# A transformer kernel whose first mixer keeps its tokens by grid columns, so that neighbourhood attention scores 128 queries with two key blocks and the context

## The chip, the cores and the metric

The kernel runs on one core of one Trainium2 chip. A core has five engines that run their own instruction streams and wait for each other by semaphores: TensorE (PE: matrix products into PSUM), VectorE (DVE), ScalarE (ACT), GpSimd (POOL) and SyncE (SP, which only issues DMAs here). The metric is the device time of one execution in microseconds, lower is better. The kernel before takes 2480.74 us, the median of 3 runs (2480.32 to 2481.86).

## What is computed

Two blocks follow one another on 512 tokens of width 1024. The second has two layers; it also carries 256 context tokens. The change touches the mixer of its first layer (`even_mixer`), which runs two attentions on halves of the width:

```python
qa, ka, va, qb, kb, vb = split(h @ w_in)               # 512 latent tokens and 256 context tokens
ya = neighbourhood_attention(rms(qa), rms(ka), va, ka_ctx, va_ctx, rpb)     # 8 heads of 64
yb = diff_attend(rope(rms(qb)), rope(rms(kb)), vb, ...)                     # 4 pairs of heads, all 768 keys
y  = concat([ya, rms(yb)]) @ w_out

# neighbourhood_attention: the 512 tokens are a grid of 8 rows and 64 columns, token = 64*row + column
row_start = clip(row - 4, 0, 8 - 8)                    # = 0: the window takes all 8 rows
col_start = clip(col - 8, 0, 64 - 16)                  # 16 columns
s = concat([q . k[window] * scale + rpb[row offset, column offset], q . k_ctx * scale])
out = softmax(s) @ concat([v[window], v_ctx])
```

So a latent query sees 8 x 16 = 128 latent keys, in a band of grid columns, and all 256 context keys. The context tokens attend to the 256 context keys alone.

## The kernel before

Activations lie with the channels on the 128 partitions and the tokens along the free dimension: 8 tiles of 512 latent and 256 context columns (`T` = 768). Dense layers multiply weights and activations in three products of high and low parts (lines 274 to 276 and, for the values, 356 to 358). Weight units stream through a ring of 4 slots: SP loads them (L3075), ACT makes the high part (L267), POOL the low part (L3124).

The program goes through stages in a fixed order that all engines follow by hand-written waits. Around the change these are: modulation `mod_a0` (DVE scales x at L595, ACT adds the shift at L611, DVE makes the low part at L589; PE multiplies tile by tile as they come, L274 to L276), the projection of the diff half (`Projection`, DVE rotates with `rope_vector` L631 to L633 and divides by the norm L755 to L760, values leave PSUM at L380), its attention, the projection of the neighbourhood half, its attention, the product with `w_out_e`, and the residual update (L1274).

Neighbourhood attention is `RowTiledAttention` over 24 "pairs". A pair is 128 queries of two heads, one head on each half of the partitions. For each of the 4 head pairs `t` there are six in this order: two blocks of context queries against 256 keys, then four blocks of latent queries against all 768 keys. With tokens by rows every block of 128 queries (two grid rows) needs all 512 latent keys; what lies outside the window is masked by the bias table. So 256 of the 768 key columns are context and 384 of the other 512 are masked for each query.

The steps of pair `p`, by engine:
- PE `score` (L1072): one product for each head and 256 keys, into PSUM. The profile counts two records for each product in fp32.
- DVE `largest` (L1180 and L1182): the maximum. A wide pair takes two instructions for each head: 256 context columns with a zero bias, then 512 with the bias table.
- ACT `exp` (L1148), DVE reciprocal (L1168), POOL scaling of the probabilities (L1015).
- PE `turn` (L1090): transposes into PSUM banks 6 and 7, which hold one phase of at most 8 blocks; ACT copies them out (L1136). A pair of 12 blocks turns in two phases, the first ("opening") at step `p+2`, the second ("closing") at step `p+3`. Each turn waits until the phase before is copied.
- PE `sum` (L1109): values times probabilities, at step `p+4`; DVE stores the result (L1187).

One step of the PE loop is: `sum(p-4)`, closing turn of `p-3`, `score(p)`, opening turn of `p-2`. In a wide pair `score` also waits before its second chunk for the store of pair `p-4`. DVE at its step `p` does `largest(p)` for head 0, the reciprocals of `p-1`, the store of `p-3` and `largest(p)` for head 1; ACT does its first exp, then the closing copy, then its second exp. After some steps DVE also prepares the bias table of a head (L1718: 14 x 64 = 896 columns, at the first two pairs of each `t`) or a lower part of the mix (L1251), and ACT its high part (L1244). At the end PE fills in three products with `w_out_e` beside the last pairs. The bias tables come by 16 DMAs of 64 partitions x 14 rows x 256 bytes (L3175), 12 of them issued after the projection.

Of the kernel before, what the change touches and what calls it, by code (L numbers as in the profile page):

```python
# [14 lines left out]
P = 128  # L15
D = 1024
DT = D // P
S = 512
# [12 lines left out]
WIN_R, WIN_C = 8, 16  # L31
EMB, ORDER = 33, 64
# [29 lines left out]
for _name, _n in PARAMS:  # L62
# [6 lines left out]
          ("later", P), ("upto", P), ("na_mask", GRID_W), ("cos", S), ("sin", S)]  # L69
# [512 lines left out]
def modulate_vector(k, v, name, layer, shift0, lo, n):  # L582
# [46 lines left out]
def rope_vector(k, v, x, xs, gain, gain_swap):  # L629

    link(v, v.eng.scalar_tensor_tensor(x, x, gain, k.const("cos", 0, S), ALU.mult, ALU.mult))  # L631
    link(v, v.eng.scalar_tensor_tensor(xs, xs, gain_swap, k.const("sin", 0, S), ALU.mult, ALU.mult))
    v.eng.tensor_tensor(x, x, xs, ALU.add).then_inc(k.sem("head_rotated"), 1)  # L633


class Projection:
# [5 lines left out]
    def __init__(self, k, name, tiles, values, units, width, dst, before, evacuated, rotated, turned, jobs):  # L642
# [3 lines left out]
        self.evac, self.backward = k.sem("head_evac"), turned  # L646
# [42 lines left out]
    def scalar(self, s):  # L689
        k, n = self.k, self.tiles  # L690

        def square(i):
# [8 lines left out]
            blocks = (lambda ap: ap.rearrange("p (b n) -> p b n", n=P)) if i < self.backward else (lambda ap: ap)  # L701
            back = (lambda ap: blocks(ap)[:, :, ::-1]) if i < self.backward else (lambda ap: ap)
            s.eng.activation(back(k.sq[:, i % 2, 0:size]), blocks(src), ACT.Square).then_inc(self.squares, 1)

        def keep(i):
# [8 lines left out]
            if i < self.backward:  # L714
                x, src = x.rearrange("p (b n) -> p b n", n=P)[:, :, ::-1], src.rearrange("p (b n) -> p b n", n=P)
# [27 lines left out]
    def vector(self, v):  # L743
        k, n = self.k, self.tiles
        for events in self.slots:
            for j in events:
                x, _, gain, _, _, gain_swap = self.jobs[j]
                size = x.shape[-1]
                if gain_swap is not None:
                    v.eng.wait_ge(self.evac, self.e + j + 1)  # L750
                    rope_vector(k, v, x[:, 0:S], swapped(k, j), gain, gain_swap)
# [15 lines left out]
class PairAttention:  # L767
# [5 lines left out]
    def __init__(self, k, pairs, third, before, opened, wide=(0, 0, 0)):  # L773
# [9 lines left out]
        self.wide = [sum(it["keys"].shape[-1] > S for it in pairs[:p]) for p in range(len(pairs) + 1)]  # L783
# [27 lines left out]
    def score_at(self, p, h):  # L811

        base = 1536 * (p % 2)
        return base if h == 0 else base + (768 if self.pairs[p]["keys"].shape[-1] > S else 512)

    def probs(self, p, h):
        n = self.pairs[p]["keys"].shape[-1]
# [23 lines left out]
    def score(self, pe, p):  # L841
        k, it = self.k, self.pairs[p]
        self.open(pe, "score", p)
        n = it["keys"].shape[-1]
# [32 lines left out]
    def sum(self, pe, p):  # L877
# [6 lines left out]
        for b, val in enumerate(it["values"]):  # L884
            if it["joined"]:
                last = pe.matmul(k.ps[:, out:out + P], val, self.probs_turned(p, b, b + 1), start=b == 0, stop=b == n - 1)
            else:
                for h in range(2):
                    r, g = slice(HD * h, HD * h + HD), h * n + b
                    last = pe.matmul(k.ps[r, out:out + P], val[:, r], self.probs_turned(p, g, g + 1), start=b == 0,  # L890
# [27 lines left out]
    def scalar(self, s, between=None):  # L918
# [8 lines left out]
        def exp(p, h):  # L927
            it, n = self.pairs[p], self.pairs[p]["keys"].shape[-1]
# [19 lines left out]
    def vector(self, v, between=None):  # L948
# [12 lines left out]
        def largest(p, h):  # L961
            it, n, at = self.pairs[p], self.pairs[p]["keys"].shape[-1], self.score_at(p, h)
# [5 lines left out]
            w, least = it["bias"][h].shape[-1], -MASKED  # L968
# [54 lines left out]
class RowTiledAttention(PairAttention):  # L1023
# [31 lines left out]
    def score(self, pe, p):  # L1055
        k, it = self.k, self.pairs[p]
        self.open(pe, "score", p)
        n = it["keys"].shape[-1]
# [5 lines left out]
        for a in range(0, n, CTX):  # L1064
            b = min(a + CTX, n)
# [4 lines left out]
            for h in range(2):  # L1070
                r, at = slice(HD * h, HD * h + HD), self.score_at(p, h)
                last = pe.matmul(k.ps[:, at + a:at + b], it["q"][r], it["keys"][r, a:b], start=True, stop=True)  # L1072
# [2534 lines left out]
```

## Time and profile before

| | us |
|---|---|
| median of 3 runs | 2480.74 |
| profiled execution, span | 2478.6 |
| mod_a0 with its first products | 767 to 787 |
| diff projection | 787 to 883 |
| diff attention | 883 to 966 |
| neighbourhood projection | 966 to 1082 |
| neighbourhood attention | 1082 to 1175 |
| product with w_out_e | 1175 to 1242 |

The times of the stages are microseconds from the start of the span, read off the timeline. The profile shows one execution: "busy" is the time in which an engine had an instruction under way. PE records overlap (a matmul's record lasts longer than the distance to the next), so a group of matmuls is best read by its first start and the next group's start. PEclk is the clock that TensorE was granted, as a share of 2.4 GHz.

### The profile page before, as it was taken

What the parts mean: (1) busy time and instruction counts of PE and PEld (TensorE: products, weight loads), DVE (VectorE), ACT (ScalarE), POOL (GpSimd) and SP (SyncE); (2) the same over time, 40 slices, a digit from 0 to 9 for tenths busy, and PEclk for the clock granted to TensorE, in tenths of its full rate; (3) what the DMA queues carried; (4) which work ended last, traced back from release to release, by engine and by line L of the source; (5) the groups of instructions that cost most, each with busy time, mean ns of one, the idle gap of its engine ahead of it and who ended that gap; (6) DMA issues with size and microseconds to landing.
All of it is one profiled execution on the core that took longest, in us unless ns stands there. A gap on an engine that the chain in (4) does not pass through costs nothing.

```text
span 2478.6 us, 37835 instructions
## 1 busy us (share of the span) xinstructions
PE 2426.4 (98%) x14711; PEld 1982.5 (80%) x14711; DVE 1512.1 (61%) x2120; ACT 974.5 (39%) x1541; POOL 829.5 (33%) x446
## 2 busy tenths in 40 slices
PE   8999999999999999999999999999999999999999
PEld 6778877888886877777888888888887757788887
DVE  6765755458567975696366866644777587424242
ACT  4576643232325455357242122132256332423232
POOL 2533033544441222233223323232223322354443
PEclk9999999999999999999999999999999999999999
DMA  6222023445431101130123433322311111233232
GB/s 248 86 68 77 3 68 126 146 144 172 151 127 41 53 26 33 52 79 2 60 94 114 158 127 126 121 94 91 129 62 56 53 67 54 83 114 97 94 102 85
DMA packets 78682, 228.53 MB, mean 92 GB/s; under 512 B 21568, under 2 KB 23616, under 8 KB 77898
## 3 DMA queue, kind: packets, MB, share of 16 engines
q1 hardware_dynamic: 65176, 177.12, 21.9%
q10 hardware_dynamic: 13362, 49.40, 6.0%
q8 instruction: 102, 1.67, 0.3%
q14 instruction: 42, 0.34, 0.0%
HBM read 224.37 MB, written 2.12 MB: 91 GB/s over the span
## 4 chain that ended last, share of the span: by engine, by line
PE 84%; DVE 7%; issue 4%; ACT 2%; POOL 2%; DMA 0%; SPq 0%; DVEq 0%; POOLq 0%; ACTq 0%
PE ps L274 23%; PE ps L275 23%; PE ps L276 22%; PE ps L1109 2%; PE ps L1072 2%; POOL w_lo L3124 1%; PE ps L1090 1%; PE ps L856 1%; DVE rstd L755 1%; PE ps L873 1%; PE ps L358 1%; PE ps L356 1%; PE ps L357 1%; PE ps L468 1%; PE ps L2896 1%
## 5 line engine op out<-in xcount | busy, mean ns | idle before, releaser
L3124 POOL TENSOR_TENSOR w_lo<-ring,w_hi 128x1024 fp32r<-128x1024 f32 x288 | 703.5, 2443 | 1163.9 <-ACT w_hi L267 661.1
L274 PE MATMUL ps<-act_hi,w_hi 128*128 128x512 f32 x2280 | 843.6, 370 | 4.8 <-DVE act_lo_mixer L589 2.4
L276 PE MATMUL ps<-act_hi,w_lo 128*128 128x512 f32 x2280 | 828.6, 363 | 0.0
L275 PE MATMUL ps<-act_lo_ffn,w_hi 128*128 128x512 f32 (+1 forms) x1408 | 512.9, 364 | 0.0
L274 PEld LDWEIGHTS ps<-act_hi,w_hi 128*128 128x128 f32 x2280 | 429.1, 188 | 93.0 <-issue 16.5
L276 PEld LDWEIGHTS ps<-act_hi,w_lo 128*128 128x128 f32 x2280 | 428.1, 188 | 71.9
L267 ACT CAST w_hi<-ring 128x1024 fp32r<-128x1024 f32 (+1 forms) x167 | 172.6, 1034 | 653.8 <-PE ps L276 604.7
L1471 ACT CAST w_hi<-ring 128x1024 fp32r<-128x1024 f32 (+1 forms) x132 | 137.6, 1043 | 457.4 <-PE ps L276 457.4
L1363 DVE SCALAR_TENSOR_TENSOR ada_place<-ada_place 128x1024 f32<-128x1024 f32 x180 | 284.6, 1581 | 25.4 <-DMA ada_place<-in_w_ada 10.5
L275 PEld LDWEIGHTS ps<-act_lo_ffn,w_hi 128*128 128x128 f32 x1408 | 265.1, 188 | 41.1
L274 PE MATMUL ps<-hidden_hi,w_hi 128*128 128x512 f32 x704 | 256.5, 364 | 1.8 <-DVE hidden_lo L1554 1.5
L275 PE MATMUL ps<-hidden_lo,w_hi 128*128 128x512 f32 x704 | 256.5, 364 | 0.0
L276 PE MATMUL ps<-hidden_hi,w_lo 128*128 128x512 f32 x704 | 255.2, 363 | 0.0
L1554 DVE TENSOR_TENSOR hidden_lo<-probs,hidden_hi 128x512 f32 (+3 forms) x66 | 150.0, 2273 | 63.7 <-ACT hidden_hi L1497 63.7
L1552 DVE TENSOR_TENSOR probs<-probs,ps 128x512 f32<-128x512 f32 (+1 forms) x66 | 51.3, 777 | 208.4 <-PE ps L276 200.7
L274 PEld LDWEIGHTS ps<-hidden_hi,w_hi 128*128 128x128 f32 x704 | 132.6, 188 | 25.0 <-DVE hidden_lo L1554 2.4
L276 PEld LDWEIGHTS ps<-hidden_hi,w_lo 128*128 128x128 f32 x704 | 132.3, 188 | 21.9
L275 PEld LDWEIGHTS ps<-hidden_lo,w_hi 128*128 128x128 f32 x704 | 132.6, 188 | 20.5
L275 PE MATMUL ps<-act_lo_mixer,w_hi 128*128 128x512 f32 (+1 forms) x416 | 147.3, 354 | 0.0
L1539 DVE SCALAR_TENSOR_TENSOR probs<-ps,params,probs 128x511 f32<-128x511 f32 x66 | 43.6, 661 | 133.0 <-ACT probs L1486 132.0
L755 DVE RECIPROCAL rstd<-probs 128x768 f32<-128x768 f32 x20 | 99.0, 4949 | 41.8 <-ACT probs L732 41.7
L1591 DVE SCALAR_TENSOR_TENSOR x_res<-ps,mod,x_res 128x512 f32<-128x512 f32 x72 | 47.7, 662 | 124.5 <-PE ps L276 123.3
(446 smaller groups left out, 3311.2 us busy)
## 6 DMA issues: line engine op xcount, KB each, us to landing
ring<-in_w_ffn SPq DMA_DIRECT2D x204, 512.0 KB, 3.3
ada_place<-in_w_ada ACTq DMA_DIRECT2D x90, 512.0 KB, 4.1
ring<-in_w_gdn SPq DMA_DIRECT2D x16, 512.0 KB, 3.3
ring<-in_w_hy SPq DMA_DIRECT2D x12, 512.0 KB, 3.3
ring<-in_w_dil_qk SPq DMA_DIRECT2D x8, 512.0 KB, 8.7
ring<-in_w_out SPq DMA_DIRECT2D x8, 512.0 KB, 3.3
ring<-in_w_diff_qk SPq DMA_DIRECT2D x8, 512.0 KB, 3.3
ring<-in_w_na_qk SPq DMA_DIRECT2D x8, 512.0 KB, 3.2
```

What stands on the lines that cost most here:

```text
L267: s.eng.copy(k.w_hi[:, u % SPLITS, rest], k.ring[:, u % SLOTS, rest]).then_inc(k.hi_done, 1)
L274: pe.matmul(out, w[0], x[0], start=start, stop=False)
L275: pe.matmul(out, w[0], x[1], start=False, stop=False)
L276: return pe.matmul(out, w[1], x[0], start=False, stop=stop)
L755: link(v, v.eng.reciprocal(k.rstd[:, 0:size], k.probs[:, j % 2, 0:size]))
L1072: last = pe.matmul(k.ps[:, at + a:at + b], it["q"][r], it["keys"][r, a:b], start=True, stop=True)
L1109: last = pe.matmul(k.ps[r, out:out + P], val[:, r], self.probs_turned(p, g, g + 1), start=b == 0, stop=b == n - 1)
L1363: ins = v.eng.scalar_tensor_tensor(k.ada[:, 4, :], k.ada[:, 2 + n % 2, :], 1.0, k.ada[:, q, :], ALU.mult, ALU.mult, accum_out=k.mod_flat[: ...
L1471: s.eng.copy(k.w_hi[:, (u + j) % SPLITS, rest], k.ring[:, (u + j + 2) % SLOTS, rest]).then_inc(k.hi_done, 1)
L1552: v.eng.tensor_tensor(tmp[:, 0:n], tmp[:, 0:n], k.ps[:, val:val + n], ALU.mult).then_inc(f.hidden, 1)
L1554: v.eng.tensor_tensor(k.hid_lo[:, it * 2 + a, 0:n], tmp[:, 0:n], k.hid_hi[:, it * 2 + a, 0:n].bitcast(F32), ALU.subtract).then_inc(f.ready, 1)
L3124: pool.tensor_tensor(k.w_lo[:, a % SPLITS, :], k.ring[:, a % SLOTS, :], k.w_hi[:, a % SPLITS, :].bitcast(F32), ALU.subtract).then_inc(k.lo ...
```

## The change

Before the first layer's mixer the latent tokens are put in column order (token = 8*column + row): `modulate_vector` reads x and the norm by columns and writes them contiguously, RoPE reads its cosine and sine tables by columns, and the residual update reads the product from PSUM back into row order. The context tokens stay. In this order 128 queries starting at token 64 + 128*i are 16 grid columns, and their windows lie within 32 grid columns, that is 256 keys. The latent queries of a head pair become three blocks of 128 against 256 + 256 keys, and one pair that holds the first 64 and the last 64 queries, each half against its own 128 keys and the 256 context keys (384 in all). One instruction now takes the maximum over latent and context keys, with a bias table that holds zeros for the context. The tables (5 x 256 columns for two heads) are laid out on the host and come in one DMA for each `t`. The reversed order of queries that the old table needed is gone. A pair of 4 or 3 blocks turns in one phase (8 or 6 blocks), at step `p+3`.

```diff
@@ modulate_vector
+    turned = name == "mod_a0"
     for t in range(DT):
         for q, (a, b) in enumerate(parts):
-            ins = v.eng.scalar_tensor_tensor(bufs[t % 3][:, a:b], k.x[:, t, a:b], k.mod[:, layer, shift0 + 8 + t, q:q + 1],
-                                             norm_rstd(k, v, name, q), ALU.mult, ALU.mult)
+            dst, src, rstd = bufs[t % 3][:, a:b], k.x[:, t, a:b], norm_rstd(k, v, name, q)
+            if turned and q == 0:
+                dst, src, rstd = in_columns(dst), by_columns(src), by_columns(rstd)
+            ins = v.eng.scalar_tensor_tensor(dst, src, k.mod[:, layer, shift0 + 8 + t, q:q + 1], rstd, ALU.mult, ALU.mult)
@@ rope_vector
+    cos, sin = k.const("cos", 0, S), k.const("sin", 0, S)
+    if columns:
+        cos, sin, x, xs = by_columns(cos), by_columns(sin), in_columns(x), in_columns(xs)
@@ Projection: squares and copies of the queries no longer reverse blocks of 128
@@ RowTiledAttention.score
-        for a in range(0, n, CTX):
-            b = min(a + CTX, n)
+        for c, (a, b) in enumerate(zip([0] + it["ends"], it["ends"])):
...
             for h in range(2):
                 r, at = slice(HD * h, HD * h + HD), self.score_at(p, h)
-                last = pe.matmul(k.ps[:, at + a:at + b], it["q"][r], it["keys"][r, a:b], start=True, stop=True)
+                for rows, q, keys in it["pieces"]:
+                    last = pe.matmul(k.ps[rows, at + a:at + b], q[r], keys[c][r], start=True, stop=True)
@@ RowTiledAttention.sum
-                last = pe.matmul(k.ps[r, out:out + P], val[:, r], self.probs_turned(p, g, g + 1), start=b == 0, stop=b == n - 1)
+                for cols, v in val:
+                    last = pe.matmul(k.ps[r, out + cols.start:out + cols.stop], v[:, r], self.probs_turned(p, g, g + 1)[:, cols],
+                                     start=b == 0 and cols.start == 0, stop=b == n - 1, skip_group_check=len(it["pieces"]) > 1)
@@ largest
+            bias = it["bias"][h]
+            if len(bias.shape) == 3:
+                chunks = lambda ap: ap.rearrange("p (a n) -> p a n", n=bias.shape[-1])
+                v.eng.tensor_tensor_reduce(chunks(self.probs(p, h)), chunks(k.ps[:, at:at + n]), bias, 1.0, -MASKED,
+                                           ALU.add, ALU.min, self.small(p, 0, h)).then_inc(self.maxed, 1)
+                return
@@ residual_vector
+            if name == "w_out_e" and q == 0:
+                x, src = x.rearrange("p (r c) -> p r c", c=GRID_W), back_in_rows(src)
@@ new helpers
+def by_columns(ap):
+    return ap.rearrange("p (r c) -> p c r", c=GRID_W)
+def in_columns(ap):
+    return ap.rearrange("p (c r) -> p c r", c=GRID_W)
+def back_in_rows(ap):
+    return ap.rearrange("p (c r) -> p r c", c=GRID_W)
+def na_table(k, t):
+    return k.view(k.mix_flat, 5 * T, 5, CTX) if t == 0 else k.view(k.big, 12 * T + 5 * CTX * t, 5, CTX)
@@ na_pairs
-        for i in (4, 5, 0, 1, 2, 3):
...
-                out.append(pair(q[:, t, blk], key[:, t, 0:T], vals, k.mix[:, 4 + t, blk][:, ::-1],
-                                bias=[bias[2 * t + h][:, at:at + S] for h in range(2)]))
+        for i in (4, 5):
+            blk = slice(i * P, (i + 1) * P)
+            out.append(pair(q[:, t, blk], ctx, vals[4:], mix[:, blk], bias=[k.par("zero").broadcast_to([P, CTX])] * 2))
+        for i in range(3):
+            blk = slice(HD + i * P, HD + (i + 1) * P)
+            out.append(pair_of([(slice(0, P), q[:, t, blk], [key[:, t, i * P:i * P + CTX], ctx])], whole[i:i + 2] + whole[4:],
+                               mix[:, blk], bias=[table[:, 0::3, :], table[:, 1:4:2, :]]))
+        low, high, units = slice(0, HD), slice(HD, P), table.rearrange("p a (u n) -> p (a u) n", n=P)
+        out.append(pair_of([(low, q[:, t, 0:HD], [key[:, t, 0:P], ctx]), (high, q[:, t, S - HD:S], [key[:, t, S - P:S], ctx])],
+                           [[(low, vals[0]), (high, vals[3])]] + whole[4:], ...))
@@ na_mask_vector
-        link(v, v.eng.scalar_tensor_tensor(bias, bias, -1.0,
-                                          k.const("na_mask", 0, GRID_W).unsqueeze(1).broadcast_to([P, 14, GRID_W]),
-                                          ALU.mult, ALU.add))
+            edges = na_table(k, t)[:, 2, :]
+            link(v, v.eng.tensor_scalar(edges, edges, -1.0, None, ALU.mult))
+        bias = na_table(k, t)[:, h, :].rearrange("p (c r) -> p c r", c=WINDOW)
+        link(v, v.eng.scalar_tensor_tensor(bias, bias, -1.0, spread(k.const("na_mask", 0, WINDOW), ROWS_ALL), ALU.mult, ALU.add))
@@ load_na_bias
-    for h in (2 * t, 2 * t + 1):
-        for a in range(2):
-            sp.dma_start(na_bias(k)[h][GRID_W * a:GRID_W * (a + 1), :, :],
-                         bass.AP(k.dram["rpb"], (h * 15 + a) * wide, [[1, GRID_W], [wide, 14], [1, GRID_W]]))
+    sp.dma_start(na_table(k, t), k.dram["na_bias"][t]).then_inc(k.sem(f"na_bias_{t}"), 16)
```

## Rows read from the trace of the kernel before

**Rows 1.** The page: the span
```profile
span 2478.6 us, 37835 instructions
```
**Rows 2.** Windows: start:end, length, busy time by engine, PEclk, DMA share, GB/s
```profile
1108.28:1129.95 21.67, 19.24 (x284) 14.69 (x282) 17.19 (x63) 18.14 (x36) 9.03 (x13) 1.00 0.01 2
1129.95:1151.17 21.22, 19.17 (x283) 14.65 (x282) 16.30 (x62) 17.52 (x35) 9.10 (x13) 1.00 0.01 3
```
**Rows 3.** The chain that ended last, in order of time: start, us, what
```profile
1092.40 0.66 PE ps L1109 x8
...
1129.95 1.35 PE ps L1072 x12
...
1139.09 0.59 PE ps L1090 x12
...
1142.18 1.46 PE ps L1109 x24
...
1173.60 1.46 PE ps L1109 x24
```
**Rows 4.** Timeline, turns on PE and their copies on ACT: start, us, what
```profile
1133.70 0.56 ACT L1136 COPY pair_turned<-ps 128x512 f32<-128x512 f32 x1
...
1134.46 0.45 PEld L1109 LDWEIGHTS ps<-pair_turned,big 128*64 128x64 f32 x8 [0.36 <-ACT pair_turned L1136]
...
1150.59 0.59 PE L1090 MATMUL ps<-consts,act_place 64*128 64x64 f32 x12
...
1151.21 0.80 ACT L1136 COPY pair_turned<-ps 128x768 f32<-128x768 f32 x1 [0.68 <-PE ps L1090]
...
1153.91 0.46 PE L1090 MATMUL ps<-consts,probs 64*128 64x64 f32 x8
```
**Rows 5.** Groups by form, 1084 to 1174: names, shapes, count, busy, mean ns, idle before
```profile
L1148 ACT ACTIVATE act_place<-act_place,small 128x768 f32<-128x768 f32 x16 | 15.0, 939 | 4.9 <-DVE small L1182 4.8
L1148 ACT ACTIVATE probs<-probs,small 128x256 f32<-128x256 f32 x8 | 4.1, 512 | 0.1
L1182 DVE CUSTOM_DVE_ANT_0 act_place<-ps,big,small 128x512 f32<-128x512 f32 x12 | 9.0, 751 | 0.4
L1180 DVE CUSTOM_DVE_ANT_0 act_place<-ps,params 128x256 f32<-128x256 f32 x16 | 6.7, 419 | 3.2 <-PE ps L1072 2.0 <-DVE big L1718 1.0
```
**Rows 6.** Timeline, the first bias tables on DVE and POOL beside them
```profile
1084.18 2.37 POOL L3124 TENSOR_TENSOR w_lo<-ring,w_hi 128x1024 fp32r<-128x1024 f32 x1 [7.52 <-ACT w_hi L267]
...
1084.41 3.08 DVE L1718 SCALAR_TENSOR_TENSOR mix<-mix,consts 128x896 f32<-128x896 f32 x1
...
1088.34 1.21 DVE L1718 SCALAR_TENSOR_TENSOR mix<-mix,consts 128x896 f32<-128x896 f32 x1
```
**Rows 7.** DVE forms of the whole span: a strided PSUM read, and L595 of mod_a0
```profile
L3051 DVE SCALAR_TENSOR_TENSOR mix<-ps,small,mix 128x512 f32<-128x512 f32 x4 | 3.0, 744 | 0.1
L595 DVE SCALAR_TENSOR_TENSOR sq<-x_res,mod,ps 128x512 f32<-128x512 f32 x24 | 17.9, 744 | 4.6 <-PE ps L458 4.5
L595 DVE SCALAR_TENSOR_TENSOR sq<-x_res,mod,ps 128x256 f32<-128x256 f32 x18 | 8.5, 475 | 0.0
```
**Rows 8.** The same kind of window over mod_a0 and its first products
```profile
767.00:787.00 20.00, 18.81 (x96) 14.77 (x95) 18.80 (x32) 9.38 (x17) 1.35 (x1) 1.00 0.01 1
```
**Rows 9.** Timeline of DVE in the diff projection
```profile
811.31 2.10 DVE L759 TENSOR_TENSOR big<-big,rstd 128x512 f32<-128x512 f32 x1
...
876.60 0.69 DVE L380 COPY big<-ps 128x512 f32<-128x512 f32 x1 [5.08 <-PE ps L358]
```
**Rows 10.** Timeline, the end of the attention, and DVE in the product after it
```profile
1175.43 2.70 DVE L1251 TENSOR_TENSOR mix_lo<-mix,act_hi 128x768 fp32r<-128x768 f32 x3
...
1205.82 1.27 DVE L1274 SCALAR_TENSOR_TENSOR x_res<-ps,mod,x_res 128x512 f32<-128x512 f32 x2 [4.07 <-PE ps L276]
```
**Rows 11.** Windows where the granted clock fell
```profile
249.00:252.00 3.00, 1.10 (x14) 0.47 (x9) 2.74 (x3) 2.41 (x6) 0.00 (x0) 0.93 0.00 0
252.00:255.00 3.00, 3.00 (x42) 2.11 (x42) 2.93 (x3) 0.93 (x4) 0.00 (x0) 0.50 0.00 0
```

More of the change, by code:

```diff
@@ L31 @@
 WIN_R, WIN_C = 8, 16
+WINDOW = 32
+ROWS_ALL = S // GRID_W
+assert WIN_R == ROWS_ALL
 EMB, ORDER = 33, 64
@@ L782, in __init__ @@
         self.joined = [sum(it["joined"] for it in pairs[:p]) for p in range(len(pairs))]
-        self.wide = [sum(it["keys"].shape[-1] > S for it in pairs[:p]) for p in range(len(pairs) + 1)]
+        self.wide = [sum(it["n"] > S for it in pairs[:p]) for p in range(len(pairs) + 1)]
         count, N = dict(self.first), len(pairs)
@@ L843, in score @@
         self.open(pe, "score", p)
-        n = it["keys"].shape[-1]
+        n = it["n"]
         if p >= 2:
@@ L927, in exp @@
         def exp(p, h):
-            it, n = self.pairs[p], self.pairs[p]["keys"].shape[-1]
+            it, n = self.pairs[p], self.pairs[p]["n"]
             if h == 0 and p >= 3:
@@ L961, in largest @@
         def largest(p, h):
-            it, n, at = self.pairs[p], self.pairs[p]["keys"].shape[-1], self.score_at(p, h)
+            it, n, at = self.pairs[p], self.pairs[p]["n"], self.score_at(p, h)
             if it["bias"] is None:
@@ L1057, in score @@
         self.open(pe, "score", p)
-        n = it["keys"].shape[-1]
+        n = it["n"]
         if p >= 2:
@@ L1063, in score @@
                 pe.wait_ge(self.maxed, 2 * self.nth(p - 1))
-        for a in range(0, n, CTX):
-            b = min(a + CTX, n)
+        for c, (a, b) in enumerate(zip([0] + it["ends"], it["ends"])):
             if a == S:
@@ L1071, in score @@
                 r, at = slice(HD * h, HD * h + HD), self.score_at(p, h)
-                last = pe.matmul(k.ps[:, at + a:at + b], it["q"][r], it["keys"][r, a:b], start=True, stop=True)
+                for rows, q, keys in it["pieces"]:
+                    last = pe.matmul(k.ps[rows, at + a:at + b], q[r], keys[c][r], start=True, stop=True)
             if a == 0 and n > S:
@@ L1097, in sum @@
         self.copies_ready(pe, self.phases[p][-1].copies)
-        if p + 2 < len(self.pairs) and self.pairs[p + 2]["keys"].shape[-1] > S:
+        if p + 2 < len(self.pairs) and self.pairs[p + 2]["n"] > S:
             if self.pairs[p + 2]["bias"] is None:
@@ L1141, in exp @@
         def exp(p, h):
-            it, n = self.pairs[p], self.pairs[p]["keys"].shape[-1]
+            it, n = self.pairs[p], self.pairs[p]["n"]
             if h == 0 and p >= 3:
@@ L1170, in largest @@
         def largest(p, h):
-            it, n, at = self.pairs[p], self.pairs[p]["keys"].shape[-1], self.score_at(p, h)
+            it, n, at = self.pairs[p], self.pairs[p]["n"], self.score_at(p, h)
             if it["bias"] is None:
@@ L1641, in pair, with pair_of @@
 def pair(q, keys, values, out, bias=None, factor=None):
-    return dict(q=q, keys=keys, values=values, blocks=len(values), out=out, bias=bias, factor=factor,
-                joined=factor is not None)
+    chunks = [keys[:, a:min(a + CTX, keys.shape[-1])] for a in range(0, keys.shape[-1], CTX)]
+    return pair_of([(slice(0, P), q, chunks)], [[(slice(0, P), val)] for val in values], out, bias, factor)
+def pair_of(pieces, values, out, bias, factor=None):
+    return dict(pieces=pieces, ends=list(itertools.accumulate(ap.shape[-1] for ap in pieces[0][2])), n=len(values) * P, values=values,
+                blocks=len(values), out=out, bias=bias, factor=factor, joined=factor is not None)
 def dil_pairs(k):
@@ L1666, in na_pairs @@
 def na_pairs(k):
     q, key, val = attn_views(k)
[L1668 removed]
+    out = []
     for t in range(4):
[L1670 to L1678 removed]
+        vals, mix, table = [val[:, b, t * P:(t + 1) * P] for b in range(6)], k.mix[:, 4 + t, :], na_table(k, t)
+        whole, ctx = [[(slice(0, P), v)] for v in vals], key[:, t, S:T]
+        for i in (4, 5):
[7 more added lines that the diff above has]
+        out.append(pair_of([(low, q[:, t, 0:HD], [key[:, t, 0:P], ctx]), (high, q[:, t, S - HD:S], [key[:, t, S - P:S], ctx])],
+                           [[(low, vals[0]), (high, vals[3])]] + whole[4:],
+                           mix[:, 0:S].rearrange("p (e n) -> p e n", n=HD)[:, ::S // HD - 1, :], bias=[units[:, 4:9:2, :], units[:, 5:10:2, :]]))
```

88 lines of the change are left out of this document (41 added, 47 removed).

## The prediction

> **What bounds the kernel now.** I read the page first: the span is 2478.6 us [rows 1], the median of the runs 2480.74, so 2.1 us lie outside the span; I keep them and make the sum against the span. The change touches four stages, so I read windows and timelines of those. In neighbourhood attention one group of six pairs takes 21.67 and then 21.22 us, with PE busy for 19.2, ACT for 17.5 to 18.1 and DVE for 16.3 to 17.2 of it [rows 2]. PE leads, but the others stand close behind: removing PE work alone would buy little, and what matters is that the change shrinks the work of all of them. The chain in order of time [rows 3] then gives PE's parts: a score of 768 keys 1.35 us, a turn of 6 blocks 0.59, a sum of 12 blocks 1.46; a context pair has a turn of 0.46 [rows 4] and a sum of 0.66 [rows 3]. From the first sum at 1092.40 to the end of the last at 1173.60 + 1.46 = 1175.06 there are 82.7 us, 24 steps of the PE loop. This is the stretch to be rebuilt.
>
> **Neighbourhood attention, PE.** An interior pair scores 512 columns instead of 768 (0.90 us), turns 8 blocks in one phase (16 records instead of 12 and 12: 0.79) and sums 8 instead of 12 blocks (0.97). The pair of edges scores 384 columns, turns 6 blocks (0.59) and sums 6 (0.73). Its score consists of products on a quarter of the array; if quarters don't overlap it costs up to 1.28, and I show below that this is covered. Context pairs stay: 0.45, 0.46, 0.62 to 0.66.
>
> **What PE waits for in a step.** The turn's PSUM region is free, and the sum has its input, only after ACT's copy. A turn that ended at 1151.18 was followed by the copy at 1151.21, and a copy that ended at 1134.26 by the sum's first load at 1134.46 [rows 4]: 0.03 + copy + 0.20. The copies of 512 and 768 columns took 0.56 and 0.80 [rows 4], 0.94 ns for a column, so 1024 columns cost 1.04. Round trips are thus 0.79, 1.04 and 1.27 us. Only the score lies beside them. A step is sum + turn + the larger of score and round trip. After the change, by p modulo 6:
> - 0 and 1: 0.97 + 0.79 + 1.27 = 3.03 each
> - 2: 0.97 + 0.59 + 1.04 = 2.60
> - 3: 0.73 + 0.46 + 0.90 = 2.09
> - 4: 0.62 + 0.46 + 0.90 = 1.98
> - 5: 0.62 + 0.79 + 1.27 = 2.68 (the edge score, even at 1.28, fits beside the copy)
>
> That is 15.4 us a group. The same reckoning for before (with the second turn and its wait for the first copy) gives 3.68 twice, 3.40, 3.27, 3.02 and 3.15, together 20.2, where the trace has 21.2 to 21.7 [rows 2]; it leaves out 1.0 to 1.5 us of couplings between engines, so I price these for after by themselves. Steps 4 and 5 of the first group (4.66), three groups (46.2) and the tail (steps 24 to 27, each with a product of w_out_e of about 1.27 where the score was: 3.03, 3.03, 2.83, 0.73) make 60.5 us against 82.7: 22.2 less.
>
> **Couplings.** ACT: exps of 768 and 256 columns take 0.94 and 0.51 [rows 5], so 512 take 0.72; its step with two of them and the large copy is 2.5 us, below 3.03. DVE: 419 + 751 ns for each head become one instruction over 512 columns, 751 ns [rows 5], about 0.80 with its accumulator read; reciprocals and store take some 0.5 a step (what maxima, two tables of 1.09 and a low part leave of DVE's 17.19 us a group [rows 2], over six), so a step is 2.1. POOL was busy 9.03 us for the 7168 columns of a group [rows 2], so an interior pair takes 1.3; the turn is now always two steps behind the exps and finds it done, where the opening turn of before waited for it. The weak place is step 3 of the groups in which DVE makes a lower part of the mix (2.70 us for three [rows 10], so 0.9 to 1.1 beside its 2.1) while PE's steps are only 2.0: the next maximum comes late, the exp after it stands ahead of the large copy on ACT, and behind that copy PE waits. Written out, the copy starts 1.3 us late. Two groups have this; the others lose about 0.25, and ACT's casts of the mix in two places 0.35 each. Sum: 2 x 1.3 + 2 x 0.25 + 2 x 0.35 = 3.8 us back.
>
> **Fill.** The first two bias tables took DVE 3.08 and 1.21 us; the first ran into POOL's low part, which ended at 1084.18 + 2.37 = 1086.55 [rows 6]. The new table work is 256 + 256 columns and then 256; it will still have to wait for POOL, and ends perhaps 0.2 us sooner, the second 0.7, and the following pair saves 0.56 on its maxima. The first sum starts about 1.4 us sooner. Later tables shrink as well, within DVE's steps counted above.
>
> The attention comes to -22.2 - 1.4 + 3.8 = -19.8 us. Next late behind it is the product with w_out_e. It starts with tiles prepared long before; DVE's last three low parts took 2.70 us from 1175.43 [rows 10] and move with the end of the attention. Its weights were in the ring by then (the DMA is idle from 1108 on [rows 2]), so the gain isn't eaten there.
>
> **mod_a0.** DVE is busy for 18.80 of the 20 us [rows 8] and PE's products follow it tile by tile, so every nanosecond on its 8 instructions of L595 is exposed. They now read x and the norm with a hop of 64 words at each element. A row shows that a hop at every element in PSUM costs nothing: L3051 takes 744 ns for 512 columns, just as the contiguous L595 [rows 7]. No row shows such a read from SBUF. One bound is therefore 0. The other: a column costs (744 - 475) / 256 = 1.05 ns [rows 7], and if each took two turns, 0.54 us for each of 8 instructions, 4.3 us. I take the middle, 2.1, since x hops in SBUF and the norm in PSUM. The Trainium skill (Vector Engine (DVE) Microarchitecture Reference, Measured stream behaviour on trn2) says that hopping one source at every element raises 1.054 to 1.73 ns for a column, and stepping both by 24 words to 2.50; by it the eight would cost an estimated 2.8 to 5.9 us. No run here shows it yet.
>
> **Cover elsewhere.** RoPE: two of three instructions in 8 jobs now hop in SBUF, at worst 2 x 0.54 = 1.1 us a job. In each job the multiplication L759 takes 2.10 us, where the copy of as many columns takes 0.69 [rows 9], because it runs beside POOL's low part, so up to 1.4 us of delay vanish there; and after the last job DVE idles 5.08 us before the values [rows 9]. I cost it at nothing; without that cover it would be 8.6 us minus 5. The residual reads PSUM with a hop (nothing, by rows 7), and DVE waits 4.07 us for PE there anyway [rows 10]. Squares and copies without the reversal, and 3 DMAs instead of 12 on SP: nothing, since the queue isn't waited for.
>
> **The sum.** -19.8 + 2.1 = -17.7: span 2460.9, time 2480.74 - 17.7 = 2463.0 us.
>
> **Rivals.**
> - *The steps don't follow PE but the loop between engines* (store, maximum, exp, copy, sum runs over two steps). For it speaks that before was 1.0 to 1.5 us a group above PE's reckoning. If after loses 2.5 us a group beyond it (18 us instead of 15.4) the saving is 22.2 + 1.4 - 4 x 2.5 = 13.6, less mod_a0: -11.5, 2469.2. Chance 0.22.
> - *A hop in SBUF costs more than a second turn*: with three turns an element, 8 x 1.08 = 8.6 us in mod_a0, and RoPE at 2.2 us a job breaks its cover of 1.4 by 0.8 x 8 = 6, of which the 5.08 of idle time hide most: -19.8 + 8.6 + 1 = -10.2, 2470.5. Chance 0.09. The Trainium skill's upper figure (same page and section) stands between this and my bound.
> - *More than forecast*: couplings vanish and the hops are free, -22.2 - 1.4 = -23.6, 2457.1; if PE's parts overlap a little more, 2455. Chance 0.1.
> - *Slower: TensorE's clock falls.* PE is busy 90% now; after it would be 13.4 of 16.4 us, 82%, with gaps of up to 0.4 us at each large copy. In this trace the granted clock fell to 0.50 (1.2 GHz) in the three microseconds after a window in which PE was busy for 1.10 of 3 us [rows 11]. If gaps bring it down and it stays, PE work doubles: the stretch holds about 54 us of it, so it costs 54 us minus the waits that it hides (12), against 20 saved: +22, 2503. It decides from about 40% of the stretch at the lower level. Against it: no gap here comes near that one. Chance 0.03.
> - *The gain is eaten*: the product with w_out_e waits for weights or low parts, within 5 us of before. Rows 10 and the idle DMA speak against it. Chance 0.05.
>
> **Numbers.** The forecast has 0.50. Its own range, from the bounds of the hops and 3 us on the couplings either way, is 2458 to 2468. The 8 in 10 take in the first rival: 2456 to 2471. About 0.2%, 5 us, is what a measurement here can tell. Faster by more: 0.91, same 0.05, slower 0.04.
>
> **What would show it.** Right: groups of six pairs in 15.4 to 16.5 us; the turn of 16 records at 0.79 followed by a copy of 1.04 and a PE gap of some 0.3; first sum near 1091 plus the shift of mod_a0; L595 at about 1.0 us; the RoPE stage unchanged in length because L759 shrinks by what L631 and L632 grow; w_out_e of the same length. Wrong: steps of equal length near 3 us (the loop), PEclk below 1.00 in the attention, PE idle before L274 of w_out_e, or a longer diff projection.

## The result, and the profile after

The changed kernel takes 2461.49 us (median of 4, 2459.59 to 2464.36), the kernel before 2481.19 beside it: a ratio of 0.9922 (0.991 to 0.9933), 19.7 us faster where 17.7 were forecast. The profiled execution is the slowest of the four, 2464.36 us with a span of 2462.4.

The window of the kernel after from the first sum's start to the last sum's end (columns as in [rows 2]):

```profile
1093.05:1154.38 61.33, 53.30 (x803) 39.27 (x803) 41.04 (x165) 50.87 (x116) 26.81 (x44) 1.00 0.07 29
```

The 82.66 us of before are now 61.33, a group takes 16.06 us twice and then 15.08 instead of the 21.2 and 21.7 of [rows 2], and the clock stays at 1.00. The chain that ended last, in order of time (start, us, what), has the two kinds of step in it:

```profile
1117.73 0.66 PE ps L1101 x16
1118.42 1.02 ACT pair_turned L1149
1119.48 1.09 PE ps L1121 x16
1120.58 0.52 PE ps L1101 x12
1121.10 0.92 PE ps L1083 x8
1122.02 0.87 PE ps L1121 x16
1123.28 0.95 PE ps L1083 x8
1124.39 0.48 issue
1125.12 1.38 POOL act_place L1026 x2
1126.55 0.65 issue
1127.21 0.54 DVE pair_probs L1193
1127.99 0.81 ACT pair_probs L1161 x2
1128.80 0.91 ACT pair_turned L1149
1129.75 1.09 PE ps L1121 x16
1130.85 0.66 PE ps L1101 x16
1131.53 1.02 ACT pair_turned L1149
1132.59 1.09 PE ps L1121 x16
```

L1121 is the sum, L1101 the turn, L1149 ACT's copy, L1083 the score. Up to 1122.02 and again from 1129.75 the chain alternates between TensorE and the large copy: that is the step of the forecast. Between them it leaves TensorE and runs over POOL, DVE, the exponential and the copy. The timeline of that place:

```profile
1125.97 1.32 DVE L1272 TENSOR_TENSOR mix_lo<-mix,act_hi 128x768 fp32r<-128x768 f32 x1
1127.21 0.68 DVE L1193 CUSTOM_DVE_ANT_1 pair_probs<-ps,big 128x512 f32<-128x512 f32 x1
1127.62 0.88 PE L1083 MATMUL ps<-big 64*64 64x128 f32 x16
1129.75 1.09 PE L1121 MATMUL ps<-pair_turned,big 128*64 128x128 f32 x16 [1.25 <-ACT pair_turned L1149]
```

The low part of the mix (L1272) begins while POOL is still scaling (until 1126.48) and keeps the maximum (L1193) back, the exponential after it stands ahead of the copy on ACT, and PE is idle for 1.25 us. The edge pair's score has 16 records and takes 0.88 us: it fits beside the copy.

Where the 20 us are, taken from the first modulation read (767.14 before, 766.93 after), which leaves out what the executions differ by at the start:

| | before | after | difference | forecast |
|---|---|---|---|---|
| modulation stage, first read to last low part's start | 16.18 | 18.76 | +2.6 | +2.1 |
| from there to the first sum | 309.08 | 307.36 | -1.7 | -1.4 |
| first sum to end of last | 82.66 | 61.33 | -21.3 | -18.4 |
| end of last sum to end of span | 1303.5 | 1308.0 | +4.5 | 0 |

The first three make -20.5. Of these 4.5 us are lost again in stages that the change doesn't touch. Windows of after over the end of the w_out_e stage and the norm behind it:

```profile
1220.00:1223.00 3.00, 2.72 (x15) 2.25 (x15) 0.01 (x1) 2.33 (x3) 2.21 (x1) 0.75 0.00 0
1223.00:1226.00 3.00, 3.00 (x11) 2.61 (x12) 0.19 (x1) 0.27 (x1) 0.00 (x0) 0.50 0.54 175
1226.00:1229.00 3.00, 3.00 (x11) 2.19 (x11) 2.00 (x4) 0.69 (x2) 0.00 (x0) 0.62 0.00 0
```

The granted clock falls to 0.50 (1.2 GHz). In the place that corresponds (1239 to 1251) before has 1.00 throughout. A second such place is 2030 to 2045 (0.89 after, 1.00 before in 2045 to 2060). Runs below show that this comes and goes.

### The profile page after: what moved, and what is told of

The parts are those of the page before. It is cut to its first block, busy times and chain, and to the rows that moved or that the text cites. A ratio compares the mean times of both kernels' runs of the same rounds, so it can differ in the third digit from the quotient of the medians.

```text
span 2462.4 us, 37109 instructions
## 1 busy us (share of the span) xinstructions
PE 2406.9 (98%) x14407; PEld 1965.0 (80%) x14407; DVE 1494.2 (61%) x2060; ACT 957.7 (39%) x1525; POOL 820.7 (33%) x446
## 3 DMA queue, kind: packets, MB, share of 16 engines
q1 hardware_dynamic: 51160, 176.05, 21.3%
## 4 chain that ended last, share of the span: by engine, by line
PE 84%; DVE 7%; issue 4%; ACT 3%; POOL 2%; DMA 0%; SPq 0%; DVEq 0%; POOLq 0%; ACTq 0%
PE ps L277 23%; PE ps L278 23%; PE ps L279 22%; PE ps L1121 2%; POOL w_lo L3172 1%; PE ps L861 1%; PE ps L1083 1%; DVE rstd L760 1%; PE ps L1101 1%; PE ps L878 1%; PE ps L361 1%; PE ps L360 1%; PE ps L359 1%; PE ps L471 1%; PE ps L2944 1%
## 5 line engine op out<-in xcount | busy, mean ns | idle before, releaser
L277 PEld LDWEIGHTS ps<-act_hi,w_hi 128*128 128x128 f32 x2280 | 429.7, 188 | 97.6 <-issue 17.7
L278 PEld LDWEIGHTS ps<-hidden_lo,w_hi 128*128 128x128 f32 x704 | 132.6, 188 | 20.5
```

Of the source, the lines that this page charges most:

```text
L277: pe.matmul(out, w[0], x[0], start=start, stop=False)
L278: pe.matmul(out, w[0], x[1], start=False, stop=False)
```

## The experiments

The theory (A): a step is sum + turn + the larger of score and copy round trip; the low part in front of the edge pair is the one large coupling; the read that hops costs what it costs in its own stage; and (C) the loss after the attention is the clock of single executions. Rivals: (B) a loop through DVE, ACT and POOL sets the pace; (D) the change itself moves something in the later stages, each time. The measure for A and B is the distance from the start of the first sum to the start of the last (60.43 us in the profile after), read off each run's timeline; whole times of single runs spread by 5 us. The three whole groups are steps 6 to 11, 12 to 17 and 18 to 23 of the PE loop, from the start of one sum to that of the next.

**The changed kernel again.**

> The changed kernel again, for its spread. After's profile shows the attention ending 20.7 us sooner against the start of the span, but the span is only 16.2 us shorter: in three places behind it the granted clock is below 1.00 where the kernel before had it at 1.00 (windows 1220 to 1229: 0.75, 0.50, 0.62). Theory C (these falls come and go from one execution to the next): the runs spread over some 5 us, from about 2459.5 to 2464.5, and a run with a mean granted clock of 0.998 is about 2460, one of 0.996 about 2464, so that a thousandth of clock goes with about 2.3 us. Rival (a loss that the change brings each time, such as another place of a transfer): runs within 1 us of each other, whatever the clock.

2462.61 us (2458.04 to 2462.95), ratio 0.992 (0.9906 to 0.9933); distance 60.40 us. The runs spread over 4.9 us, as C says. **And once more**, in another set:

> The changed kernel again, for the run before this one to be held against: 2461 to 2463 us in the median, single runs between 2458 and 2465, the longer ones with the lower mean clock (0.996 against 0.998).

2462.9 us (2458.11 to 2463.08), ratio 0.9925 (0.9911 to 0.9938); distance 60.40 us. Its profiled run is the one of 2458.11 us, and its windows at the same place are:

```profile
1220.00:1223.00 3.00, 3.00 (x24) 2.82 (x24) 0.34 (x2) 1.01 (x3) 0.56 (x1) 1.00 0.43 120
1223.00:1226.00 3.00, 2.74 (x8) 0.96 (x6) 2.80 (x5) 1.89 (x4) 0.00 (x0) 1.00 0.14 55
1226.00:1229.00 3.00, 2.37 (x13) 2.12 (x14) 2.96 (x7) 1.45 (x3) 0.00 (x0) 1.00 0.00 0
```

It has no fall there, and from the end of its last sum (1151.84 + 0.90 = 1152.74) to the end of its span (2456.1) it takes 1303.4 us, as before does (1303.5). That rules D out as a loss that comes each time: the stages behind are as fast as they were when the clock stays up. Windows of 5 us over all that follows the last sum show falls at three places, some 65 to 75, 630 to 650 and 870 to 880 us behind it. Of the eleven profiles of the changed kernel and its variants two have only the middle one, as before has (0.80 and 0.86 there), and take 1303.4 to 1303.5 us; five have the middle one and one of the others and take 1304.8 to 1305.8; four have all three, the profile above among them, and take 1307.9 to 1308.0. Whether the first and the last are more frequent than before isn't settled: the one profile of before hasn't got them, but the runs of before spread by 5 us as well (2478.25 to 2483.33 in nine).

**Turn and copy in two halves.** TURNED decides from how many blocks on a pair is turned in two phases.

```diff
-TURNED = 8
+TURNED = 6
```

> The changed kernel with a limit of 6 instead of 8 blocks a phase, so that interior pairs turn in two phases of 4 blocks, one at step p+2 and one at p+3; the copies are of 512 columns. Theory A (a step is sum + turn + the larger of score and copy round trip): the second copy hides beside the sum, the first beside the score; steps 0, 1 and 5 of a group fall from about 2.85 to 2.2 to 2.6, steps 2 and 3 stay, step 4 grows by 0.4; 1.0 to 1.4 us a group, 4 to 5.5 us in all, 2455 to 2457. Rival B (the loop through store, maximum, exp and copy sets the pace): the same time or up to 2 us more, since ACT has one more instruction a pair and PE waits for POOL one step sooner, 2461 to 2463.

2459.55 us (2458.05 to 2461.82), ratio 0.9914 (0.99 to 0.9927); distance 60.43 us, no shorter. The steps of the first whole group, with the later runs beside them (us; p as in the forecast), and of the third whole group, in which neither DVE's low parts nor ACT's casts of the mix lie:

| p modulo 6 | 0 | 1 | 2 | 3 | 4 | 5 | group |
|---|---|---|---|---|---|---|---|
| forecast, without couplings | 3.03 | 3.03 | 2.60 | 2.09 | 1.98 | 2.68 | 15.41 |
| after | 2.95 | 2.84 | 2.51 | 2.40 | 1.99 | 3.37 | 16.06 |
| two halves | 3.09 | 2.17 | 3.04 | 2.40 | 2.44 | 2.94 | 16.08 |
| later low part | 2.94 | 2.85 | 2.51 | 2.40 | 1.99 | 2.59 | 15.28 |
| halves and later low part | 3.08 | 2.17 | 3.04 | 2.41 | 2.42 | 2.40 | 15.52 |
| halves, second on DVE | 3.05 | 4.14 | 2.50 | 2.41 | 2.43 | 3.77 | 18.30 |
| POOL scales half | 2.95 | 2.84 | 2.51 | 2.40 | 1.99 | 3.00 | 15.69 |
| after, third group | 2.84 | 2.85 | 2.50 | 2.31 | 2.08 | 2.50 | 15.08 |
| two halves, third group | 2.61 | 2.17 | 2.51 | 2.30 | 2.53 | 2.39 | 14.51 |

In the first group steps 1 and 5 get 0.67 and 0.43 shorter, and steps 2 and 4, with 0 a little, longer by as much. What PE waited for, of after (1093 to 1154) and then of this run (1091 to 1152; engine, line, releaser: us in total, times, longest):

```profile
PEld ps L1121 <- ACT pair_turned L1149: 17.0, 22, 1.7
...
PEld ps L1101 <- issue: 3.8, 22, 0.2
```
```profile
PEld ps L1121 <- ACT pair_turned L1149: 6.3, 10, 0.9
...
PEld ps L1101 <- issue: 7.7, 26, 0.7
...
PEld ps L1101 <- POOL probs L1026: 2.6, 4, 0.9
```

Most of the wait for the copy has gone, and waits ahead of the turn have come, for POOL's scaling among them: an opening turn runs a step sooner and finds the probabilities not yet scaled. A turn in one phase waits for the copy, a turn in two for the loop, and in the first two groups both give 16.1 us. In the third group, where DVE and ACT have less to do, the halves do bring something, 0.57 us (15.08 to 14.51), and the tail behind the groups and the two steps ahead of them lose it again (0.36 and 0.16). That the whole distance is the same to 0.01 us is thus chance. A is right on what sets the steps of this kernel, and wrong on what taking it away would give (1.0 to 1.4 us a group were expected); B holds the moment the copy lets go, in the groups with low parts and casts.

**The low parts of the mix one step later.** Two of DVE's low parts (1.32 us each beside POOL, 0.96 alone) move one step later: DVE made them two steps ahead of the edge pair's own step (11 and 17), and now makes them one step ahead.

```diff
-    if p in (6, 9, 12, 15):
-        mix_split_vector(k, v, "mix_e", T, ((p - 6) // 3,), (p - 6) // 3)
+    if p in (6, 10, 12, 16):
+        t = (6, 10, 12, 16).index(p)
+        mix_split_vector(k, v, "mix_e", T, (t,), t)
```

> The changed kernel, with two of DVE's low parts of the mix made one step later (after steps 10 and 16 instead of 9 and 15). In the chain of the changed kernel PE waits 1.25 us for the copy at step 5 of these groups, behind an exp that came late behind such a low part, and the low part itself ran into POOL's scaling. Theory A: the wait of about 1.3 us goes in both groups, 2 to 2.6 us less, unless the low part meets POOL and the maxima of the edge pair as badly at its new place. Rival (the late copy has another cause, such as ACT's own queue): no difference.

2459.55 us (2457.93 to 2460.38), ratio 0.9914 (0.9899 to 0.9929); distance 58.88 us, 1.5 shorter. All of it is in step 5 of two groups, 3.37 to 2.59 (the table): the coupling foretold at this place is real, at 0.78 us instead of 1.3. (The third group of after, with no low part at all, has 2.50 there.) The edge pair's step still waits for its copy, for 0.48 us instead of 1.25:

```profile
1126.61 1.09 PE L1121 MATMUL ps<-pair_turned,big 128*64 128x128 f32 x16 [0.48 <-ACT pair_turned L1149]
```

At its new place the low part isn't held up (0.97 us); POOL's scalings beside it are, and take 2.13 us for the two instead of 1.36:

```profile
1124.92 2.13 POOL L1026 TENSOR_SCALAR probs<-probs,small 128x512 f32<-128x512 f32 x2 [0.80 <-DVE small L1181]
...
1125.60 0.97 DVE L1272 TENSOR_TENSOR mix_lo<-mix,act_hi 128x768 fp32r<-128x768 f32 x1
```

The same kernel again, in one set with the second repeat of the changed kernel:

> The kernel with the low parts of the mix after steps 10 and 16, again, beside the changed kernel on the same chip. Its stretch of sums is 1.5 us shorter; if that reaches the end, its median lies 1.5 us under the changed kernel's (with falls of the clock in the wide stages moving single runs of either by up to 5 us, between 0 and 3 us under it). If what ends the attention sooner is lost again later in the kernel, there is no difference.

2458.6 us (2458.24 to 2460.07), ratio 0.9913 (0.9899 to 0.9926), against 2462.9 for the changed kernel; distance 58.88 against 60.40. The medians differ by more than the 1.5 us that the change explains; three of the five runs beside it had the lower clock, 0.997, and the fastest runs of both lie together (2458.24 and 2458.11). The profile of this kernel has 1.7 us more behind the attention than that of the changed one (1305.1 against 1303.4), with a granted clock of 0.88 in 1218 to 1232 where the other has 1.00. So the distance shows the 1.5 us, twice; whole times agree with it, without showing it. By the distance it is the fastest version that I have.

**Both edits together.**

> The changed kernel with both edits at once: interior pairs turned and copied in two halves of 512 columns instead of one of 1024, and VectorE's low parts of the mix placed after steps 10 and 16 instead of 9 and 15. The stretch from the first sum of the neighbourhood attention to its last sum was 60.5 us with neither, 60.5 with the halves alone and 58.95 with the later low parts alone. If a loop through VectorE and GpSimd alone sets the pace, the halves again bring nothing: 58.9 to 59.2 us. If each of the two limits hides the other (the copy round trip where VectorE is on time, VectorE where the copy is on time), taking both away brings more than their sum: 57.5 us or less, by at least 1.2 us under the later low parts alone. If ScalarE pays for the additional copies (12 more, some 0.1 us each), 59.5 us or more.

2460.79 us (2459.89 to 2463.57), ratio 0.9919 (0.9907 to 0.9931); distance 59.30 us, 0.4 more than with the later low part alone. Taking away both isn't more than the sum, so the low part's place wasn't what hid the halves' gain. Group by group the halves cost 0.24 us in each of the first two (15.52 against 15.28), bring 0.57 in the third (14.51 again), and cost 0.16 ahead of the groups and 0.35 behind them. The result lies between two of the stated cases; that the additional copies are what costs is not shown.

**The second half's copy on DVE.** The kernel of the run before with

```diff
-    na = RowTiledAttention(k, na_pairs(k), k.h_flat[:, 4 * T:6 * T], diff, first, (2, 2, 10))
+    na = RowTiledAttention(k, na_pairs(k), k.h_flat[:, 4 * T:6 * T], diff, first, (2, 2, 10), ("act", "dve"))
```

and pairs of one phase left to ScalarE.

> The kernel of the run before this one with the second half of each interior pair's copy on VectorE instead of ScalarE (12 copies of 512 columns, 0.56 us each on ScalarE). If ScalarE is the member of the loop that is short of time in the interior pairs (two exponentials of 0.72 us with their 0.11 to read the sums, and 1.0 us of copies make 2.7 us a pair, near the step's 2.54 to 2.84), the stretch gets shorter by up to 12 x 0.3 = 3.6 us against the run before this one. If VectorE is (two maxima of 0.76, inversions 0.22 and a copy of the sum 0.27 make 2.0 us, with the copy on top 2.7), the stretch gets longer, by 1 to 4 us, since what ScalarE gains VectorE loses. If TensorE's own work sets the pace, nothing changes (within 0.3 us).

2468.24 us (2467.49 to 2470.52), ratio 0.9951 (0.9938 to 0.9963); distance 68.30 us, 9.0 more. ScalarE isn't what is short; the loop through DVE is, and by more than foretold. The copy (0.68 us on DVE, against 0.56 on ACT) stands at the head of DVE's step, behind the work that DVE adds after the step before and ahead of both maxima. Step 1 grows from 2.17 to 4.14 and step 5 from 2.40 to 3.77. In step 1 PE's turn was over at 1119.39, and DVE came to its copy after two instructions for the bias table and a low part:

```profile
1120.38 0.96 DVE L1272 TENSOR_TENSOR mix_lo<-mix,act_hi 128x768 fp32r<-128x768 f32 x1
1121.26 0.68 DVE L1149 COPY pair_turned<-ps 128x512 f32<-128x512 f32 x1
```

DVE's busy time is only 46.64 of 69.21 us: it isn't full, but late. And in this run a rival of the forecast shows itself that nowhere else did: the timeline of TensorE after a gap of 2.16 us, and the windows there:

```profile
1122.04 1.09 PE L1121 MATMUL ps<-pair_turned,big 128*64 128x128 f32 x16 [2.16 <-issue]
...
1123.61 2.02 PE L1083 MATMUL ps<-big 64*128 64x256 f32 x8
```
```profile
1121.00:1124.00 3.00, 1.96 (x30) 1.82 (x32) 2.24 (x10) 0.75 (x3) 0.94 (x2) 0.89 0.00 0
1124.00:1127.00 3.00, 3.00 (x26) 1.97 (x26) 0.98 (x5) 2.31 (x5) 0.36 (x1) 0.55 0.02 5
```

The clock falls to 0.55 for 3 us, and a score of 8 records takes 2.02 us instead of 1.08. This is at most 1.7 of the 9.0 us (3 x 0.11 + 3 x 0.45). An equal gap one group earlier (2.15 us, ahead of the sum at 1103.75) had no fall behind it: the clock is 1.00 in 1100 to 1110.

**Half of POOL's scaling.** 256 of the 512 probability columns of the interior pairs stay unscaled.

```diff
+                part = self.probs(p, h)
+                if isinstance(self, RowTiledAttention) and it["n"] == S:
+                    part = part[:, 0:CTX]
-                pool.tensor_scalar(self.probs(p, h), self.probs(p, h), ...)
+                pool.tensor_scalar(part, part, ...)
```

> The changed kernel, with GpSimd scaling only 256 of the 512 probability columns of each head of an interior pair; the other 256 columns stay unscaled, so that this part of the computation is left out. It takes some 0.34 us from each of 24 scalings of 0.70 us. If GpSimd's scaling stands in the loop that sets the pace (by the way of VectorE's inversion, the scaling and then the turn), each interior pair gets shorter by up to 0.34 to 0.68 us and the stretch from the first to the last sum by 4 to 8 us. If the copy round trip or VectorE sets it, the stretch shrinks by less than 1 us: only what VectorE's two-operand work beside GpSimd stretches (0.96 us alone against 1.31 beside it, four times) comes back, up to 1.2 us.

2462.74 us (2459.61 to 2463.81), ratio 0.9922 (0.9906 to 0.9938); distance 59.69 us, 0.74 less. POOL's busy time fell from 26.81 to 21.56 us, and only step 5 moved, 3.37 to 3.00, in two groups. This is the second case of the expectation: DVE's low part there takes 0.37 us less, all that the step gained (there are two such meetings with POOL, not the four of the expectation):

```profile
1125.51 0.95 DVE L1275 TENSOR_TENSOR mix_lo<-mix,act_hi 128x768 fp32r<-128x768 f32 x1
```

It was 1.32 beside the whole scaling. So POOL costs time here by holding up that DVE instruction, about half of the 0.78 us of the low part's place, and not as a link of the loop ahead of the turn, although the chain above goes through it.

**The modulation reads in rows.** The three operands are left in row order, so the mixer gets its tokens in the wrong order; the work is the same.

```diff
-            if turned and q == 0:
-                dst, src, rstd = in_columns(dst), by_columns(src), by_columns(rstd)
```

> The changed kernel, but the modulation reads x and the norm contiguously (tokens stay in rows there, so this leaves the reordering out). L602 took 1.12 us with hops and 0.74 without. If DVE sets the end of this stage, all eight differences are exposed: 3.0 us less. Rival: PE, with about 2.1 us of products a tile against DVE's 2.2, hides part of it, 1.5 us or less.

2459.36 us (2458.06 to 2459.64), ratio 0.9912 (0.9897 to 0.9927). DVE's pairs of instructions of mod_a0 (512 and 256 columns), after and then here (line 600 in this kernel):

```profile
771.11 1.51 DVE L602 SCALAR_TENSOR_TENSOR probs<-x_res,mod,ps 128x512 f32<-128x512 f32 x2
```
```profile
771.10 1.13 DVE L600 SCALAR_TENSOR_TENSOR probs<-x_res,mod,ps 128x512 f32<-128x512 f32 x2
```

The stage from the first of them to the last low part shrinks from 18.76 to 16.16 us, before's 16.18. From the first of them to the attention's first maximum it is 316.55 us here, 319.17 after and 316.58 before: the hop costs 2.6 us, and RoPE, which still hops in this run, costs nothing. The eight differences make 3.0; the missing 0.4 is where DVE, reading in rows, waits 0.45 us for ACT ahead of the first low part anyway. So the expectation's first case holds but for that, and PE hides nothing.

**Which hop costs.**

```diff
-                dst, src, rstd = in_columns(dst), by_columns(src), by_columns(rstd)
+                dst = (by_columns if t == 4 else in_columns)(dst)
+                src = (by_columns if t in (1, 3, 5, 7) else in_columns)(src)
+                rstd = (by_columns if t in (2, 3, 6, 7) else in_columns)(rstd)
```

> The changed kernel with the eight modulation reads of the first mixer's norm each hopping from row to row on another operand; where not all agree, the tokens come out mixed, so that part of the computation isn't the reference's. Tiles 0: nothing hops; 1 and 5: the source in SBUF alone; 2 and 6: the source in PSUM alone; 3 and 7: both; 4: the destination in SBUF alone. All eight hopping on both sources took 1.12 us each where none hopping took 0.74. If the source in SBUF alone costs, as the strided PSUM reads of the trace before that cost nothing (0.74 with and without) suggest, tiles 1, 3, 5, 7 take 1.12 and tiles 0, 2 and 6 take 0.74. If it is the pair of hops together, only 3 and 7 take 1.12. A hopping destination is in no row so far: 0.74 if only reads cost, 1.12 if writes do too.

2460.61 us (one run). Tiles 2 to 7 in order (tiles 0 and 1 are one row):

```profile
770.97 1.13 DVE L604 SCALAR_TENSOR_TENSOR probs<-x_res,mod,ps 128x512 f32<-128x512 f32 x2
...
773.20 1.52 DVE L604 SCALAR_TENSOR_TENSOR sq<-x_res,mod,ps 128x512 f32<-128x512 f32 x2
...
775.82 1.42 DVE L604 SCALAR_TENSOR_TENSOR sq<-x_res,mod,ps 128x512 f32<-128x512 f32 x2
...
778.34 1.51 DVE L604 SCALAR_TENSOR_TENSOR probs<-x_res,mod,ps 128x512 f32<-128x512 f32 x2
...
780.95 1.13 DVE L604 SCALAR_TENSOR_TENSOR sq<-x_res,mod,ps 128x512 f32<-128x512 f32 x2
...
783.18 1.51 DVE L604 SCALAR_TENSOR_TENSOR sq<-x_res,mod,ps 128x512 f32<-128x512 f32 x2
```

The PSUM source alone: 1.13 in tiles 2 and 6, nothing. The SBUF source alone: 1.51, and no more with both. The destination alone, in a single row: 1.42.

## Why the prediction was right, step by step

- *The steps of TensorE.* Right in kind: the turn, the copy, then the sum behind it. With the low part moved the six steps come to 15.28 us against 15.41; in the third group, without one, to 15.08. Steps 0, 1, 2 and 5 are then 0.1 to 0.2 shorter than foretold. Step 1 of the chain above shows by what: sum 1.02 (0.97 foretold), turn 0.71 (0.79), round trip of the copy 1.11 (1.27), since the next sum starts 0.05 us behind the copy and not 0.20. Step 3 is 0.31 longer (2.40; 2.31 in the third group). From the starts in PE's timeline its terms are 0.83 for the edge pair's sum instead of 0.73 (16 records, because its first block is summed in two halves), 0.30 for the turn, and 1.27 from the score's start to the next sum instead of 0.90, with a wait of 0.20 for a copy that stood behind an exponential on ACT.
- *Couplings.* The mis-sized term. 3.8 us were priced; the stretch from the first sum's start to the last one's end was 61.33 where the steps alone were to make 60.5, so 0.8 in all. The low part ahead of the edge pair came where and how it was written out, but at 0.78 instead of 1.3, twice (later low part). About half of that is POOL, which stretches the low part by 0.37. The other 1.2 us, for the remaining steps and ACT's casts, are hardly there: steps 0 and 3, which have a cast beside them in the first group, are 0.11 and 0.09 longer than in the third. And 0.8 is less than the two low parts' 1.56, since the steps themselves came out shorter than foretold: two errors that offset each other in part.
- *The loop as rival.* It didn't decide: 16.06 us a group, not 18. It stands just behind, though: without the copy's round trip it gives the same 16.1, and 14.5 where DVE has no low part and ACT no cast.
- *Fill.* -1.7 (309.08 to 307.36) for -1.4.
- *The hop in mod_a0.* 2.6 for 2.1: inside the bounds, above the middle. The reason given for the middle (x hops in SBUF, where it may cost, the norm in PSUM, where it doesn't) is what the last run shows, but that the middle came out near is luck, since no row gave a size; an instruction of 512 columns goes from 0.74 to 1.12 us. By the Trainium skill (Vector Engine (DVE) Microarchitecture Reference, Measured stream behaviour on trn2) one source that hops by 4 KiB at every element takes 1.73 ns a column instead of 1.054, 0.68 more, the lower end of the estimate there; (1.51 - 1.13) / 512 is 0.74, so the trace, with its hop of 64 words, agrees within a tenth. A hop in PSUM beside it adds nothing (1.52 and 1.51 against 1.51).
- *RoPE at nothing.* Right, by the cover named: L640 and L641 take 1.17 and 1.16 us, and the multiplication after the reciprocal 1.27 where it took 2.10 [rows 9]. In both kernels it ends 0.55 us behind POOL's low part (812.86 before, 815.24 after), so what the two hops add only shortens its wait:

```profile
806.53 1.17 DVE L640 SCALAR_TENSOR_TENSOR big<-big,params,consts 128x512 f32<-128x512 f32 x1
807.74 1.16 DVE L641 SCALAR_TENSOR_TENSOR mix<-mix,params,consts 128x512 f32<-128x512 f32 x1
...
812.84 2.40 POOL L3172 TENSOR_TENSOR w_lo<-ring,w_hi 128x1024 fp32r<-128x1024 f32 x1 [7.28 <-ACT w_hi L270]
...
814.52 1.27 DVE L764 TENSOR_TENSOR big<-big,rstd 128x512 f32<-128x512 f32 x1
...
878.99 0.69 DVE L383 COPY big<-ps 128x512 f32<-128x512 f32 x1 [5.07 <-PE ps L361]
```

- *Residual, end of the attention.* The residual takes 1.27 us for two as in [rows 10], and the last low parts 2.70 us from 1154.75.
- *The clock.* In the attention it stays at 1.00, so that rival fell for this kernel; the run with copies on DVE shows that it was a real one, with a fall behind one of two gaps of 2.2 us. Behind the attention single executions lose up to 4.5 us to it. The forecast had no term for that. The changed stretches gained 20.5 us and the medians 19.7 where 17.7 were foretold; the medians hold an unknown number of such falls on both sides, so that they came nearer to the forecast than the stretches is luck.

## What to carry to other kernels

Write a pipelined stage's step as sum + turn + the larger of what hides and what is hidden, and then ask of the next limit how far behind it stands: here a second limit gave the same 16.1 us in two groups of three, so removing the first brought nothing. Small work in front of the shortest step cost most here; moving it by one step was worth more than any change of the copies. An engine in the chain need not be the link that costs: halving POOL's work took time only from the DVE instruction that it held up. Where the clock falls in single runs, compare stretches of the traces and not whole times.

## What the hardware showed

- DVE, two sources and fp32: a hop of 64 words at each element costs 0.38 us on 512 columns for a source in SBUF (1.51 against 1.13 for the pair of instructions), 0.29 for the destination in SBUF (1.42, one row), nothing for a source in PSUM (1.13).
- A DVE instruction with two SBUF sources takes 0.96 us for 768 columns alone and 1.32 when it begins at 1125.97 beside a POOL scaling that ends at 1126.48; a step later it takes 0.97 and POOL's two scalings beside it 2.13 instead of 1.36.
- The same kernel has the granted clock at 0.50 for 3 us in one execution and at 1.00 in another, at the same place of the program; with the other such places it is worth up to 4.5 us.
